# Sliding-window heads in the mixing phase: value block stationary, probabilities divided by their sum ahead of the turn, output turn removed

## What is computed

```
s    = q @ k.T * scale                       # masked to the window of 128
p    = softmax(concat([s, sink]))[..., :-1]  # the sink adds to the sum only
o    = p @ v                                 # 128 queries x 64
mix  = concat(fox_out, swa_out) @ w_out
x    = LayerNorm1(alpha * x + mix)
```

## Time and profile before

| | |
|---|---|
| median of three runs | 2677.02 us (2673.73 to 2678.19) |
| the profiled execution | 2682.55 us, span 2680.7 us |
| PE busy | 2532.4 us, 94% of the span |
| DVE busy | 2277.8 us, 85% |
| ACT busy | 904.8 us, 34% |
| POOL busy | 1320.4 us, 49% |
| mixing phase | first instruction at 357.9 us, routing's first at 550.9 us |

### The profile page before, as it was taken

One profiled execution on the slowest core, in us unless ns is written; L12 is line 12 of the kernel. 1 busy time (PEld: TensorE's weight loads), 2 busy tenths in 40 slices (PEclk: granted clock), 3 DMA queues, 4 the chain that ended last, 5 costly groups with the idle time before them and its releaser, 6 DMA issues.

```text
span 2680.7 us, 45230 instructions
## 1 busy us (share of the span) xinstructions
PE 2532.4 (94%) x16925; PEld 1644.2 (61%) x17115; DVE 2277.8 (85%) x4525; ACT 904.8 (34%) x1602; POOL 1320.4 (49%) x864
## 2 busy tenths in 40 slices
PE   8999979999988888999999999999999999999996
PEld 5566546599877766564564665664664665664652
DVE  3666656669899998788998998998999999999998
ACT  2344345411144556332232232332332332332324
POOL 2110010100044441467777776776676776777762
PEclk9999979999999999999999999999999999999998
DMA  5100323310024477999999999999999999999995
GB/s 220 39 17 17 113 88 130 134 56 27 27 76 128 139 221 247 368 405 375 368 379 367 373 386 365 365 387 367 340 384 375 362 366 379 360 383 368 370 321 220
DMA packets 283584, 697.89 MB, mean 260 GB/s; under 512 B 31192, under 2 KB 113624, under 8 KB 277088
## 3 DMA queue, kind: packets, MB, share of 16 engines
q0 software_dynamic: 110592, 402.70, 39.6%
q1 hardware_dynamic: 170176, 284.77, 29.8%
q10 hardware_dynamic: 2592, 7.47, 0.8%
HBM read 631.51 MB, written 61.24 MB: 258 GB/s over the span
## 4 chain that ended last, share of the span: by engine, by line
PE 44%; DVE 15%; issue 9%; DMA 7%; POOL 2%; ACT 1%; DVEq 0%; SPq 0%; ACTq 0%; POOLq 0%
PE h_psum L1742 18%; PE o_psum L2225 12%; PE g_psum L2225 8%; PE r_t_psum L1203 4%; DMA early<-v_blocks,pick_index 3%; DVE rt_hot L1641 3%; DMA early<-u_rows,pick_index 2%; POOL early L1749 2%; DVE rt_top_u L1486 2%; PE h_psum L1250 1%; DVE early L2066 1%; DVE wide L2070 1%; DVE rt_top L1484 1%; DVE rt_hot L1651 1%; DVE rt_scores L1488 1%
## 5 line engine op out<-in xcount | busy, mean ns | idle before, releaser
L1742 PE MATMUL h_psum<-early 128*128 128x384 bf16 x5448 | 759.0, 299 | 1.2 <-DVE early L1732 0.9
L1742 PEld LDWEIGHTS h_psum<-early 128*128 128x128 bf16 x5448 | 532.5, 98 | 225.4 <-issue 2.1
L1749 POOL DMA_INDIRECT early<-u_rows,pick_index x320 | 466.8, 1459 | 203.1 <-DVE dots L2066 117.6
L1749 POOL DMA_INDIRECT early<-v_blocks,pick_index x320 | 462.6, 1446 | 192.6 <-DVE wide L2070 112.7
L2225 PE MATMUL o_psum<-v_split,w_split 128*128 128x512 bf16 x2293 | 538.4, 379 | 1.4
L2070 DVE SCALAR_TENSOR_TENSOR wide<-early,dots,wide 128x1024 f32<-128x1024 f32 x320 | 405.8, 1280 | 31.5 <-DMA early<-v_blocks,pick_index 28.7
L2066 DVE CUSTOM_DVE_ANT_0 early<-early,wide 128x1024 f32<-128x1024 f32 x320 | 388.1, 1221 | 38.2 <-DMA early<-u_rows,pick_index 35.5
L2225 PEld LDWEIGHTS o_psum<-v_split,w_split 128*128 128x128 bf16 x2304 | 225.7, 98 | 272.4 <-issue 1.1
L2225 PE MATMUL g_psum<-v_split,w_split 128*128 128x512 bf16 x1400 | 344.7, 380 | 17.3 <-DVE wide L2058 4.2
L1944 ACT ACTIVATE v_split<-early 128x512 bf16<-128x512 f32 x256 | 159.4, 624 | 327.7 <-PE o_psum L2225 311.5
L2225 PEld LDWEIGHTS g_psum<-v_split,w_split 128*128 128x128 bf16 x1536 | 150.0, 98 | 176.3 <-issue 12.0
(11 more groups left out here) (235 smaller groups left out, 3224.8 us busy)
## 6 DMA issues: line engine op xcount, KB each, us to landing
early<-v_blocks SPq DMA_DIRECT2D x256, 256.0 KB, 6.3
early<-u_blocks SPq DMA_DIRECT2D x114, 512.0 KB, 7.1
gates<-wide SPq DMA_DIRECT2D x16, 2048.0 KB, 9.7
gate<-gates SPq DMA_DIRECT2D x32, 1024.0 KB, 9.5
early<-w_query SPq DMA_DIRECT2D x8, 1024.0 KB, 5.6
gates_late<-wide SPq DMA_DIRECT2D x4, 2048.0 KB, 8.0
gate<-gates_late SPq DMA_DIRECT2D x32, 256.0 KB, 14.6
early<-w_fox SPq DMA_DIRECT2D x4, 1536.0 KB, 6.5
```

The source lines that it names most:

```text
L1742: mm = pe.matmul(bank(half)[:, 0:width * P], u_split[:, k, part, c], xs[:, first:first + width, xpart, c, :], start=(c == 0 and part == 0 ...
L1749: pool.indirect_dma_start(row, None, source, bass.IndirectOffsetOnAxis(ap=pick_index[:, tile, at:at + 1], axis=0)).then_inc(arrived, 16)
```

## The change

`values` swaps its operands: the value block of a head (128 keys x 64 dimensions) is stationary and the turned probabilities (128 columns) stream; the two heads write the two halves of the PSUM partitions, so the output comes out with dimensions on the partitions. `turn_out`, `o_rows` and the second half of `o_psum` are gone, `copy_out` reads what `values` wrote. A sum along the keys can no longer be divided out per partition after that, so `scale_out` becomes `normalise`: it scales the probabilities (two scalings of 128x256 float32, in place in SBUF) before they are turned, and `turn_probs(n)` waits for it. In DVE's loop `normalise(n+1)` stands at the end of step n, behind the stage of `norm`.

```diff
@@ turn_probs
-                    pe.wait_ge(exp_done, n + 1)
+                    pe.wait_ge(normed, n + 1)
@@ values
-                    for g in range(2):
-                        cols = slice(HEAD_DIM * g, HEAD_DIM * g + HEAD_DIM)
-                        for b in range(width // P):
-                            at = (2 * g + b) * P
-                            mm = pe.matmul(o_psum[:, 0, cols], probs_t[:, at:at + P],
-                                           sv_rows[:, first // P + b, cols], start=(b == 0), stop=(b == width // P - 1))
+                    for b in range(width // P):
+                        for g in range(2):
+                            dims, at = slice(HEAD_DIM * g, HEAD_DIM * g + HEAD_DIM), (2 * g + b) * P
+                            mm = pe.matmul(o_psum[dims, :], sv_rows[:, first // P + b, dims],
+                                           probs_t[:, at:at + P], start=(b == 0), stop=(b == width // P - 1))
                     mm.then_inc(values_done, 1)
-
-                def turn_out(n):
-
-                    pe.wait_ge(out_scaled, n + 1)
-                    pe.transpose(o_psum[:, 1], o_rows[:, :], ident).then_inc(out_turned, 1)
@@ tensor loop
-                    if 0 < n <= units:
-                        turn_out(n - 1)
@@ copy_out
-                    dve.wait_ge(out_turned, n + 1)
+                    dve.wait_ge(values_done, n + 1)
...
-                    dve.tensor_copy(near[:, t % 2, 0, j], o_psum[:, 1]).then_inc(out_high, 1)
+                    dve.tensor_copy(near[:, t % 2, 0, j], o_psum[:, :]).then_inc(out_high, 1)
@@ vector
-                def scale_out(n):
-
-                    k = n % 2
+                def normalise(n):
+
+                    k, width = n % 2, window(n)[3]
                     dve.wait_ge(exp_done, n + 1)
                     dve.tensor_tensor(row_sum[:, k], row_sum[:, k], sink_exp[:, k], ALU.add).then_inc(sum_step, 1)
                     dve.wait_ge(sum_step, n + 1)
                     dve.reciprocal(row_sum[:, k], row_sum[:, k]).then_inc(inv_made, 1)
-                    dve.wait_ge(values_done, n + 1)
                     dve.wait_ge(inv_made, n + 1)
                     for g in range(2):
-                        cols = slice(HEAD_DIM * g, HEAD_DIM * g + HEAD_DIM)
-                        scaled = dve.tensor_scalar(o_rows[:, cols], o_psum[:, 0, cols], row_sum[:, k, g:g + 1], None,
-                                                   ALU.mult)
-                    scaled.then_inc(out_scaled, 1)
+                        row = probs[:, k, g * 256:g * 256 + width]
+                        scaled = dve.tensor_scalar(row, row, row_sum[:, k, g:g + 1], None, ALU.mult)
+                    scaled.then_inc(normed, 1)
@@ vector loop
                 maxima(0)
+                normalise(0)
                 for n in range(STEPS):
                     if 0 < n <= units:
                         copy_out(n - 1)
                     if n + 1 < units:
                         maxima(n + 1)
-                    if n < units:
-                        scale_out(n)
                     if n >= NORM and (n - NORM) % PAIRS < 3:
                         norm((n - NORM) // PAIRS, (n - NORM) % PAIRS)
+                    if n + 1 < units:
+                        normalise(n + 1)
```

More of the change, by code:

```diff
@@ L733, in mix_phase @@
         probs_t = sb("probs_t", [P, 4 * P])
-        o_rows = sb("o_rows", [P, P])
         neg_max, row_sum, sink_exp = sb("neg_max", [P, 2, 2]), sb("row_sum", [P, 2, 2]), sb("sink_exp", [P, 2, 2])
@@ L740, in mix_phase @@
         t_psum = ctx.enter_context(nc.psum_tensor("mx_t_psum", [P, 4 * P], F32))
-        o_psum = ctx.enter_context(nc.psum_tensor("mx_o_psum", [P, 2, P], F32))
+        o_psum = ctx.enter_context(nc.psum_tensor("mx_o_psum", [P, P], F32))
         ln_in, keys_in, sets_in = sem("ln_in"), sem("keys_in"), sem("sets_in")
@@ L747, in mix_phase @@
         exp_done, probs_turned, turn_copied = sem("exp_done"), sem("probs_turned"), sem("turn_copied")
-        sum_step, inv_made, values_done, out_scaled = sem("sum_step"), sem("inv_made"), sem("values_done"), sem("out_scaled")
-        out_turned, out_high, out_copied = sem("out_turned"), sem("out_high"), sem("out_copied")
+        sum_step, inv_made, normed, values_done = sem("sum_step"), sem("inv_made"), sem("normed"), sem("values_done")
+        out_high, out_copied = sem("out_high"), sem("out_copied")
         eps_set, mix_done, summed, stats_done = sem("eps_set"), sem("mix_done"), sem("summed"), sem("stats_done")
@@ L909, in copy_out @@
                     t, j = n // PAIRS, n % PAIRS
-                    dve.wait_ge(out_turned, n + 1)
+                    dve.wait_ge(values_done, n + 1)
                     if j == 0 and t >= 2:
                         dve.wait_ge(mix_done, t - 1)
-                    dve.tensor_copy(near[:, t % 2, 0, j], o_psum[:, 1]).then_inc(out_high, 1)
+                    dve.tensor_copy(near[:, t % 2, 0, j], o_psum[:, :]).then_inc(out_high, 1)
                     dve.wait_ge(out_high, n + 1)
-                    dve.tensor_tensor(near[:, t % 2, 1, j], o_psum[:, 1], near[:, t % 2, 0, j], ALU.subtract
+                    dve.tensor_tensor(near[:, t % 2, 1, j], o_psum[:, :], near[:, t % 2, 0, j], ALU.subtract
                                       ).then_inc(out_copied, 1)
```

## The result

The changed kernel takes 2694.32 us (median, 2692.89 to 2695.39) beside 2676.68 us for the kernel before, run in turns with it: ratio 1.0066, 95% interval 1.0052 to 1.0079. That is +17.6 us, slower, inside the stated range; the forecast was +24.7. The profiled execution took 2694.01 us.

What follows compares the result with a forecast made beforehand. PE was taken to bound the kernel. Tiles +19.8, one more norm-stage step +1.5, start +2.9 and end -1.6 gave +22.6; with +2.1 for the clock on a median of 2677.0, 2701.7 us, range 2690 to 2716.

Steps and rivals of the forecast that it cites:

- the clock's term: Mixing phase: PE's idle time makes the granted clock fall three times, about 0.7 us each, +2.1 us.
- Removed turn: Each step: without the turn of the output, PE and the round of dependencies each gain 0.11 us.
- Values swapped: Values product in each step: PE gains between 0 and 0.34 us, taken as 0.10 because of the shape change.
- Scaling chain, 1.12: From the last exponential through sum, reciprocal and two scalings on DVE back to PE: 1.12 us added to the round.
- Start: First rounds and steps 2 to 5 of the mixing phase: together +2.9 us.
- Turns 6 to 31: Six tiles at +3.30 us each, +19.8, and one more step with the first norm stage, +1.5.
- End: Last turn to routing's first queries: 10.5 us in place of 12.06, without the old `scale_out` waits, -1.6.
- the clock's rival: Clock falls in two of three of 24 steps, +11 to +24 us over the sum, about 2717 us; chance 12%.
- POOL's rival: POOL's seven or eight subtractions each meet and block a DVE scaling: +15, about 2716 us; chance 4%.
- What the phase loses the program loses: Whole program: routing starts when the mixing phase ends, so the phase's loss passes fully into the total.
- The profiled run, about 2707: Profiled execution of the changed kernel: about 2707 us, as the earlier profiled execution was 5.5 above its median.
- the norm stages are not in the way: DVE reaches the norm stages earlier, only the plain and root steps cost: 22.2 us a tile, 2683.5 us; chance 5%.

Runs made afterwards that it cites:

- e5: The changed kernel with the two scalings of the probabilities left out and the turn waiting for the exponentials again; 2663.70 us, 0.9955 of the kernel before.
- e7: The changed kernel with one more transpose on PE in each unit but the first and `o_rows` allocated again, unused; 2698.14 us, 1.0083 of the kernel before.
- copy of the changed kernel: The changed kernel, unchanged, measured and profiled once more; 2694.84 us, 1.0063 of the kernel before.
- e6: The changed kernel with scores ahead of the turn, the norm cut into four pieces over three steps, ACT's root behind the exponentials; 2662.86 us, 0.9949 of before.
- e9: The changed kernel with one already fulfilled wait more per unit on VectorE, in `normalise`; 2700.55 us, 1.0093 of the kernel before.
- e10: The kernel before with one already fulfilled wait more per unit on VectorE, in `scale_out`; 2673.04 us, 0.9992 of the kernel before.
- e4: The changed kernel with `normalise(n+1)` ahead of the norm stage on DVE instead of behind it; 2685.38 us, 1.0039 of the kernel before.

## Why the prediction was right, and where it was not

The mechanism in the phase held: the queue on DVE, with the norm stages and the scaling in front of the turn, and PE's whole round behind that turn. That the total fell into the range is not the work of all its terms: it lies 0.3 us above the lower end of the forecast's own range (2694 to 2710), since the clock's term was too large and the rest got shorter, which had no term. The steps, with what the profile of after measured:

| distance from turn to turn, us | predicted | measured |
|---|---|---|
| stage 2 | 6.25 | 6.22 |
| transposes | 5.73 | 5.61 |
| stage 0 | 6.43 | 6.42 |
| root | 6.44 | 6.49 |
| a tile | 24.85 | 24.74 |

- *Removed turn:* 0.11 predicted, 0.11 found (`e5`, `e7`). Right.
- *Values swapped:* 0.10 predicted between 0 and 0.34; it is 0.24 less 0.09 ahead of it, 0.15. The 0.34 came from the lengths of two rows. Their distances to the next row stood in the trace of before as well: 222.22 - 221.63 = 0.59 for the new form in the forgetting heads, 473.71 - 472.88 = 0.83 for the old one. PE's plain step is 4.67, not 4.72, which accounts for 0.05 of the 0.12 in the step with the transposes, the only one that PE bounds. The trace agrees in kind with the Trainium skill's rule (TensorEngine Tiling (Array Packing), Key Properties) that a change of the tiling mode drains TensorE, if the 0.09 us before `values` are that. They are not the few tenths that I gave as the reason for 0.10.
- *Scaling chain, 1.12:* measured in the root's step of after, where nothing else is in its way:

```profile
474.91 0.20 ACT L992 ACTIVATE mx_sink_exp<-mx_sink_exp 128x2 f32<-128x2 f32 x1
475.21 0.16 DVE L924 TENSOR_TENSOR mx_row_sum<-mx_row_sum,mx_sink_exp 128x2 f32<-128x2 f32 x1 [1.58 <-ACT mx_sink_exp L992]
...
475.61 0.62 DVE L930 TENSOR_SCALAR mx_probs<-mx_probs,mx_row_sum 128x256 f32<-128x256 f32 x2
```

From the end of the exponentials, 475.11, to the turn at 476.28 it is 1.17 us: 0.10 to DVE and not 0.04, the rest as estimated.
- *Start:* +2.9 predicted. From the first scores to turn 6 it is 34.2 us after (389.0 - 354.8) and 30.9 before (388.8 - 357.9): +3.3; in the copy of the changed kernel +2.5. The 0.8 us between the two lie in step 2 (6.63 and 5.83). Up to about 372.5 us the granted clock is 0.50 in the profiles of both forms, the 1.2 GHz level, as it already was ahead of the phase (345 to 350 us), so the change did not bring it about.
- *Turns 6 to 31:* 19.8 + 1.5 = +21.3 predicted, 155.1 - 134.2 = +20.9 measured.
- *End:* -1.6 predicted, 10.6 - 12.1 = -1.5 measured.
- *Phase:* +22.6 without the clock predicted, +22.8 and (copy against copy) +21.6 measured.
- *The clock, +2.1:* over-sized. Behind the start two steps of the profile of after deviate from their pattern, and one of its copy. The first of the two, in the windows view (same columns):

```profile
428.00:431.00 3.00, 3.00 (x10) 1.04 (x12) 2.52 (x5) 1.11 (x5) 0.00 (x0) 0.53 0.00 0
```

The granted clock was 0.53 here, nearly all of it at the 1.2 GHz level, after the turn at 426.70 had waited 1.60 us. But that step took 6.37 us in place of 6.22, and the next one 5.55 in place of 5.61: the slower `mix` matmuls filled idle time. Two falls cost 0.3 us at most, not 0.7 each. This also answers the clock's rival: waits of 1.3 to 1.6 us in three steps of four brought the clock down twice behind the start, and the wait of 1.95 us in the earlier trace rows was no pattern for them.
- *POOL's rival:* its subtraction runs from 488.48 for 2.13 us in the profile of after and met no scaling; of the 64 scalings of this profile none took over 0.35 us. In `e6`, where the subtraction comes earlier in the round, it did meet an operation of the maxima (L916, 128x2): beside it that took 0.74 us in place of 0.16 (469.49 to 470.23, where the subtraction ends at 470.22), and no turn waited for it.
- *"What the phase loses the program loses":* this is the step that failed. The phase gave +22.8, the program +17.6. The sum had no term for code that isn't touched. The two waits of VectorE in routing, 2.14 and 1.98 us, stand in the profile of before, and vanished with the shorter program; `e9` and `e10` show it from both sides. Nothing in the profile of before said that the change would remove them.
- *The profiled run, about 2707:* it took 2694.01 us. The profile of before was 5.9 us above its median; that of after was not.

So of the 7.1 us between forecast and result, 1.9 lie in the phase, and they are the clock's term, 2.1 forecast and at most 0.3 found. The other 5.2 lie in the rest: about 3 of them are the longer stretch of routing with the two waits, which add up to 4.1 us of VectorE's time; about 2 are open, and the parts of the program outside the phase differ by as much between profiles of one form. Open too is why `e9` lost 5.7 us against the copy of after.

What would have been the better prediction: the same sum with the clock's falls at 0.15 us each and the product's gain from distances; it would still be about 5 us too high for the rest. The chance of 5% for "the norm stages are not in the way" (2683.5 us) stood for a state that an edit of one statement's place reaches (`e4`, 2685.4), not for one that the kernel was in.

## What to carry to other kernels

When an operation moves onto the path in front of a wait, list what is queued behind the waiting instruction on each engine: here the scores, which needed nothing of it, stood behind the turn, and moving them ahead of it was worth 22 us. A saving of PE work (here 0.26 us a step) appears only in steps in which the round of dependencies is shorter than PE's work, so spread the other engines' long work over the steps before judging the idea: the same change was +17.6 us as it stood and -14 us when ordered, 4 to 5 of them from outside the phase; what the old form would reach in its best order was not measured. And compare the untouched stages of two profiles as well: a few instructions more or fewer can move a wait in a loop far away.

## What the runs showed of the hardware that was not expected

- VectorE idled 2.1 and 2.0 us at two returns of a loop in routing, released by nothing that the profile shows. Taking out or adding 32 waits earlier in its program switched both off and on together (kernel before 4.1, with the waits added none; kernel after none, with them 3.8), with 88 packets in the queue "instruction" where they are and 77 or 78 where they aren't, and two of the packets stand beside each wait that was looked at. That the idle time is a load of instructions is my reading of this. The stretch of routing is longer by about 3 us with the waits than without them.
- Waits of PE for the scaling, 21 in 32 steps, 33.3 us in sum, brought the granted clock down only twice behind the start of the phase (0.53 over 3 us the first time), and each cost 0.15 us at most, since the slow stretch lay over work that had idle time behind it.
- A column-half product of eight passes saves 0.24 us against the row form (0.59 in place of 0.83 from start to the next matmul); 0.09 us is lost again in front of it.
